# First two attentions of two transformer blocks: steps of 128 queries of two heads instead of one

## What is computed

```python
# fox: forgetting attention, c = cumsum(log f)
s = einsum(q_i, k) * D ** -0.5 + c_q - c_k ; s = where(k_pos <= q_pos, s, NEG_INF)
o_f = softmax(s) @ v
# chunked: chunks of 64 queries, each sees itself and 8 chunks before, with a bias by distance
s = einsum(q_c, k_band) * D ** -0.5 + rel_bias[:, clip(dist)] ; s = where(valid, s, NEG_INF)
o_c = softmax(s) @ v_band
mix = concat([rms_norm(o_f), rms_norm(o_c)]) @ w_out ; x = x + rms_norm(mix)
```

## Time and profile before

| | |
|---|---|
| median of 3 executions | 1573.37 us (1571.94 to 1575.12) |
| the profiled execution | 1575.11 us, its span 1573.3 us |
| PE busy | 1535.1 us, 98% of the span |
| weight loads (PEld) | 1248.9 us, 79% |
| DVE, ACT, POOL busy | 882.4, 593.8, 245.8 us |
| mean granted clock of PE | 0.993 |
| chain that ended last | 87% of it on PE |

### The profile page before, as it was taken

One profiled execution on the slowest core, in us unless ns is written; L12 is line 12 of the kernel. 1 busy time (PEld: TensorE's weight loads), 2 busy tenths in 40 slices (PEclk: granted clock), 3 DMA queues, 4 the chain that ended last, 5 costly groups with the idle time before them and its releaser, 6 DMA issues.

```text
span 1573.3 us, 22000 instructions
## 1 busy us (share of the span) xinstructions
PE 1535.1 (98%) x7988; PEld 1248.9 (79%) x7988; DVE 882.4 (56%) x1239; ACT 593.8 (38%) x889; POOL 245.8 (16%) x273
## 2 busy tenths in 40 slices
PE   9999999999999999999999999999999999999998
PEld 6787766886887788888888678888887788888887
DVE  6434787536452644343332876747877766767323
ACT  6223434544243422222222642334764433334222
POOL 0200000015002300000000455555452000000000
PEclk9999999999999999999999999999999999999999
DMA  5532000521202232333323122322002233332321
GB/s 165 188 101 86 1 2 28 180 88 59 76 28 81 80 104 83 107 90 97 107 82 105 54 81 81 101 86 84 26 1 81 80 106 97 89 107 81 108 106 54
DMA packets 152809, 132.22 MB, mean 84 GB/s; under 512 B 6301, under 2 KB 137629, under 8 KB 152741
## 3 DMA queue, kind: packets, MB, share of 16 engines
q1 hardware_dynamic: 150836, 128.11, 26.4%
q0 software_dynamic: 848, 3.17, 0.6%
q10 hardware_dynamic: 1056, 0.00, 0.0%
HBM read 129.15 MB, written 2.12 MB: 83 GB/s over the span
## 4 chain that ended last, share of the span: by engine, by line
PE 87%; DVE 6%; ACT 2%; POOL 2%; issue 2%; DVEq 0%; ACTq 0%; POOLq 0%
PE ps L1769 24%; PE ps L1771 24%; PE ps L1770 24%; PE ps L2022 2%; PE ps L438 2%; POOL x_t L744 2%; DVE work L1259 1%; PE ps L2014 1%; PE ps L471 1%; PE ps L2033 1%; PE ps L573 1%; PE ps L2155 1%; DVE a_lo L1280 1%; DVE work L1358 1%; PE ps L1957 1%
## 5 line engine op out<-in xcount | busy, mean ns | idle before, releaser
L1769 PE MATMUL ps<-a_hi,w_hi 128*128 128x512 f32 (+2 forms) x1656 | 644.8, 389 | 14.0 <-DVE a_lo L1280 5.0
L1771 PE MATMUL ps<-a_hi,w_lo 128*128 128x512 f32 (+2 forms) x1656 | 639.8, 386 | 0.0
L1770 PE MATMUL ps<-a_lo,w_hi 128*128 128x512 f32 (+2 forms) x1656 | 639.6, 386 | 0.0
L1769 PEld LDWEIGHTS ps<-a_hi,w_hi 128*128 128x128 f32 (+1 forms) x1656 | 311.3, 188 | 86.7 <-issue 10.3
L1771 PEld LDWEIGHTS ps<-a_hi,w_lo 128*128 128x128 f32 (+1 forms) x1656 | 311.2, 188 | 64.1
L1770 PEld LDWEIGHTS ps<-a_lo,w_hi 128*128 128x128 f32 (+1 forms) x1656 | 311.3, 188 | 62.2 <-issue 0.7
L822 ACT ACTIVATE w_hi<-raw 128x2048 fp32r<-128x2048 f32 x118 | 225.8, 1913 | 345.9 <-PE ps L1771 344.1
L1232 DVE TENSOR_TENSOR w_lo<-raw,w_hi 128x2048 fp32r<-128x2048 f32 x94 | 215.2, 2290 | 245.4 <-ACT w_hi L822 245.1
L749 POOL TENSOR_TENSOR w_lo<-raw,w_hi 128x2048 fp32r<-128x2048 f32 x24 | 110.6, 4610 | 449.7 <-ACT w_hi L822 449.7
L1626 DVE TENSOR_TENSOR arena<-ps,rstd 128x512 f32<-128x512 f32 x88 | 60.1, 689 | 166.3 <-PE ps L1771 160.0
L1696 DVE RECIPROCAL rstd<-std 128x512 f32<-128x512 f32 x24 | 80.5, 3353 | 27.2 <-ACT std L1146 27.2
(11 more groups left out here) (235 smaller groups left out, 1538.1 us busy)
## 6 DMA issues: line engine op xcount, KB each, us to landing
raw<-in_w_gate_up SPq DMA_DIRECT2D x44, 512.0 KB, 4.7
raw<-in_ffn_w_up SPq DMA_DIRECT2D x44, 512.0 KB, 4.6
raw<-in_attn_w_in SPq DMA_DIRECT2D x36, 512.0 KB, 4.3
raw<-in_w_in SPq DMA_DIRECT2D x24, 512.0 KB, 4.7
raw<-in_w_down SPq DMA_DIRECT2D x22, 512.0 KB, 4.0
raw<-in_ffn_w_down SPq DMA_DIRECT2D x22, 512.0 KB, 4.1
raw<-in_w_mem_kv SPq DMA_DIRECT2D x16, 512.0 KB, 4.2
raw<-in_w_out SPq DMA_DIRECT2D x8, 512.0 KB, 3.9
```

What stands on the lines that cost most here:

```text
L1769: pe.matmul(dst, s_hi, m_hi, start=start, stop=False, skip_group_check=across)
L1770: pe.matmul(dst, s_hi, m_lo, start=False, stop=False, skip_group_check=across)
L1771: return pe.matmul(dst, s_lo, m_hi, start=False, stop=stop, skip_group_check=across)
```

## The change

A step is now 128 queries of both heads of a pair (`HeadPair`), and both attentions are one list of 32 steps, `PAIRS`, written out on every engine.

- Scores: each head's matmul has 64 rows, its own half of the partitions, and needs no padded queries; the two outputs go to two neighbouring banks. In FOX the decay is added by two matmuls of 64 rows, one for each head (`decay` now stands in rows 0, 32 and again 64, 96, and `sel_pair` replaces `sel_pad`), and the mask by two of 128 rows.
- DVE: one maximum for both heads in FOX, two fused adds in CHUNKED that read the bias where it lies; one inverse and one output product for both heads. It copies only the first head's transposes.
- ACT: two exponentials a step, and the copy of the second head's transposes (`second_out`).
- One step's scores may run two steps ahead; transposes have the banks 6 and 7 for the two heads and no second pair of banks.
- The factor 0.125 of the queries moves into the product behind the query and key tiles (now with a scalar), whose first turn is written out in both projections. The selectors are made by four selects on POOL instead of two, and PE and ACT start on five signals of the constants, not six. POOL's pad copies and its cleared pad are gone. ACT and DVE make the decay's second copy.

```diff
+        class HeadPair:
...
+                self.n, self.slot = (self.i + 1) * 128, 2 * (b % 2)
...
+                self.rows = (slice(0, 64), slice(64, 128))
+                self.scores = ps[:, 4:6, 0:self.n] if b % 2 == 0 else ps[:, 0:2, 0:self.n]
...
+                self.turned = ps[:, 6:8, 0:self.n]
...
@@ POOL
-            pool.affine_select(out=sel_col[:, :], in_=sel_col[:, :], compare_op=ALU.not_equal, fill=-1.0,
-                               base=0, pattern=[[-1, HEADS]], channel_multiplier=1).then_inc(const_step, 1)
...
+            for n, row in enumerate((0, 32, 65, 97)):
...
-            pool.memset(q_pad_1, 0.0).then_inc(pad_1_cleared, 1)
...
@@ ACT
+            act.activation(sel_pair, sel_col[:, :], ACT.Copy).then_inc(decay_ready, 1)
...
+            act.activation(decay[64:72, :], decay_made, ACT.Copy).then_inc(decay_ready, 1)
...
+            def pair_exps(t):
+
+                act.wait_ge(max_done, CREDIT + t.b + 1)
+                if t.b >= 2:
+                    act.wait_ge(turned, CREDIT + t.b - 1)
+                    act.wait_ge(recip_done, CREDIT + t.b - 1)
+                for half in range(2):
...
+            def second_out(t):
+
+                act.wait_ge(turned, CREDIT + t.b + 1)
+                act.wait_ge(values_done, CREDIT + t.b)
+                act.activation(t.probs_t[:, 1, :], t.turned[:, 1, :], ACT.Copy).then_inc(second_read, 1)
+
+            pair_exps(PAIRS[0]), pair_exps(PAIRS[1])
+            for t in PAIRS:
+                second_out(t)
+                if t.b + 2 < BLOCKS:
+                    pair_exps(PAIRS[t.b + 2])
...
@@ DVE
-                        dve.tensor_tensor(flat(ch.c * (2 * S) + (QK_1 + (first + j) * S), S), ps[:, (ch.o * 2 + j) % 4, :],
-                                          rstd[:, :], ALU.mult).then_inc(freed["dve"], 1)
-                over_chunks(dve, G[name], body, peel=int(split_ahead))
+                        dve.scalar_tensor_tensor(out=flat(ch.c * (2 * S) + (QK_1 + (first + j) * S), S),
+                                                 in0=ps[:, (ch.o * 2 + j) % 4, :], scalar=0.125 if ch.o < 2 else 1.0,
+                                                 in1=rstd[:, :], op0=ALU.mult, op1=ALU.mult).then_inc(freed["dve"], 1)
+                over_chunks(dve, G[name], body, peel=1)
...
+            pair_maxima(PAIRS[0]), pair_maxima(PAIRS[1])
+            for t in PAIRS:
+                if t.b:
+                    pair_out(PAIRS[t.b - 1])
+                first_out(t)
+                if t.b + 2 < BLOCKS:
+                    pair_maxima(PAIRS[t.b + 2])
+            pair_out(PAIRS[-1])
...
@@ PE
+            def pair_scores(t):
+
+                if t.b >= 2:
+                    pe.wait_ge(probs_done, CREDIT + t.b - 1)
+                for half, rows in enumerate(t.rows):
+                    last = pe.matmul(t.scores[:, half, :], arena[rows, t.q:t.q + 128], arena[rows, t.k:t.k + t.n],
+                                     start=True, stop=not t.decays)
+                if t.decays:
+                    for half, rows in enumerate(t.rows):
+                        pe.matmul(t.scores[:, half, :], sel_pair[rows, t.p:t.p + 1].to_broadcast([64, 128]),
+                                  decay[rows, 0:t.n], start=False, stop=False)
+                    for half in range(2):
+                        last = pe.matmul(t.scores[:, half, t.n - 128:t.n], ident_r[:, :], causal, start=False, stop=True)
+                last.then_inc(scores_done, 1)
...
+            def pair_values(t):
+
+                pe.wait_ge(turned_read, CREDIT + t.b + 1)
+                pe.wait_ge(second_read, t.b + 1)
+                pe.wait_ge(heads_done, CREDIT + t.b)
...
+            pair_scores(PAIRS[0]), pair_scores(PAIRS[1])
+            for t in PAIRS:
+                pair_turned(t)
+                if t.b + 2 < BLOCKS:
+                    pair_scores(PAIRS[t.b + 2])
+                pair_values(t)
```

More of the change, by code:

```diff
@@ L419, in pipeline @@
                     values(self.pairs - 1, 7)
[L421 to L449, removed]
-            def value(self, p, u, b):
-                return flat(p * 128 + (V_1 + (self.v + b) * HW + u // 4 * 64), 64)
-            def out(self, p, u):
-                return flat(p * 128 + (HEADS_1 + u % 4 * D + self.to + u // 4 * 64), 64)
@@ L707, in _ @@
                     .then_inc(mem_loaded, 16)
-            pool.wait_ge(vec_turned, 1)
-            pool.memset(q_pad_1, 0.0).then_inc(pad_1_cleared, 1)
-            pool.wait_ge(scores_done, CREDIT + 32)
-            with pool.Fori(0, HEADS // 2) as p:
-                for half in range(2):
-                    pool.wait_ge(max_done, p * 8 + (CHUNKED.base + 4 * half - 4))
-                    pool.tensor_copy(rel_pad[:, half, :], flat(p * (2 * S) + (REL + half * S), S))\
-                        .then_inc(rel_padded, 1)
-            pool.wait_ge(max_done, CREDIT + 64)
+            pool.wait_ge(max_done, CREDIT + BLOCKS)
             pool.memset(masks_made, 0.0).then_inc(mask_step, 1)
@@ L1372, in f @@
                         pad(units, p + 1, u // 4)
-                    elif u % 4 == 2 - units.ahead and units is FOX:
-                        pad(CHUNKED, 0, u // 4)
                 return f
@@ L1559, in _ @@
             splits("chunk_v")
-            dve.wait_ge(pad_1_cleared, 1)
-            dve.wait_ge(freed["dve"], CREDIT + G["fox_qk"].freed_end)
-            for half in range(2):
-                pad(FOX, 0, half)
             for f in range(KT):
@@ L2008, in f @@
                     n = units.number(p, u)
-                    if units is FOX and isinstance(p, int) and p == 0:
-                        pe.wait_ge(turns["mem"].read, KT)
                     pe.wait_ge(probs_done, n + 1)
@@ L2030, in f @@
                     blocks = units.keys(u) // 128
-                    if units is MEMORY:
-                        for b in range(blocks):
-                            last = pe.matmul(ps[:, 2 + u % 2, 0:units.width], units.probs_t(u)[:, b * 128:(b + 1) * 128],
-                                             units.value(p, u, b), start=b == 0, stop=b == blocks - 1)
-                    else:
-                        for b in range(blocks):
-                            last = by_column_group(ps[:, 2 + u % 2, 0:units.width],
-                                                   units.probs_t(u)[:, b * 128:(b + 1) * 128], units.value(p, u, b),
-                                                   b == 0, b == blocks - 1)
+                    for b in range(blocks):
+                        last = pe.matmul(ps[:, 2 + u % 2, 0:units.width], units.probs_t(u)[:, b * 128:(b + 1) * 128],
+                                         units.value(p, u, b), start=b == 0, stop=b == blocks - 1)
                     last.then_inc(values_done, 1)
```

135 lines of the change are left out of this document (88 added, 47 removed).

## The result

The changed kernel takes 1560.74 us (median of 4 runs, 1559.58 to 1563.09) against 1573.46 for the kernel before beside it: ratio 0.9922, 95% interval 0.9906 to 0.9938. That is 12.7 us less, where 7.5 was forecast.

| part | before | after | gained | forecast |
|---|---|---|---|---|
| first score starts at | 157.85 | 157.23 | 0.6 | 0 |
| four decay periods | 4 x 13.48 | 4 x 11.75 | 6.9 | 3.3 |
| four chunked periods | 4 x 12.85 | 4 x 10.68 | 8.7 | 5.4 |
| rest of the stage, up to the memory keys | 3.9 | 6.7 | -2.9 | -1.2 |
| everything behind | | | -1.3 | 0 |

What follows compares the result with a forecast made beforehand. TensorE was taken to bound both attentions. Gains of 3.3 (decay) and 5.4 (chunked) less 1.2 at the ends made 7.5 us: 1573.4 to 1565.9, own range 1563 to 1569.5, eight-in-ten range 1558.5 to 1575.0.

Steps and rivals of the forecast that it cites:

- The passes of the scores: TensorE's scores: three records of time for four, so 7 passes a block with decay and 6 chunked, against 10 and 8.
- The rival of whole overlap: Row halves overlap whole, five and four passes; periods 11.7 and 10.8, gain 14, total 1559.3; chance 0.12.
- The sign set for this: Two-head 512-column score, first record to decay or next operation: 1.3 us for three records, 0.9 whole overlap, 1.7 none.
- The changes of division: TensorE switching how its array is divided: four per decay step, three per chunked, each 0.10 to 0.15 us.
- The rival of dearer changes: Array division changes alone cost more: 0.20 each makes the gain 4.7, 0.285 ends it; chance 0.05 beyond 0.20.
- the serial heads: Row halves don't run side by side: about 1574.5, or 1577.5 at 0.20 per change of division; chance 0.14.
- The waits: TensorE waits for ScalarE's second-head copy: 1.3 us per decay period, 2.3 per chunked period.
- The decay loop: From transposes done through next scores, maximum, exponentials and ScalarE's copy to values: 5.5 us against TensorE's 4.2.
- The ends: Stage's start as before; last step's two-head copies and eight uncovered value blocks cost 1.2 us more, bounds -0.5 and 2.5.
- Every later stage as long as before: Sign behind the attention stage: memory keys start at about 259.5 instead of 267.0, and later stages keep their lengths.
- The rival of a falling clock: TensorE's longer waits drop its clock once a period: 13.6 us lost, 6 us slower, 1579.5; chance 0.07.
- the edits at nothing: Moved 0.125, removed pads and pad copies, selector and decay copies, GpSimd's selects: counted as no gain or loss.

Runs made afterwards that it cites:

- e1_same_half: Changed kernel with both heads' score and decay matmuls on one row half (second head's output wrong): 1586.17 us, ratio 1.0075 to the kernel before.
- e5_mask_halves: Changed kernel with the causal mask added by 64-row matmuls on each head's own row half: 1554.04 us, ratio 0.9873 to the kernel before.
- e9_changed_again: The changed kernel itself, no edit, profiled once more with five rounds: 1561.40 us, ratio 0.9920 to the kernel before.
- e8_same_half_clock: Changed kernel with both heads' scores and decays on one row half, and TensorE's waits ahead of the stage filled with unread matmuls: 1579.25 us, ratio 1.0031.
- e6: Changed kernel with ScalarE's copy between the next step's exponentials, mask on row halves, and unread matmuls filling waits before the first score: 1550.69 us, ratio 0.9849.
- e7: Changed kernel with ScalarE's copy between the next step's exponentials and the mask on row halves, without filling matmuls: 1549.93 us, ratio 0.9851.
- e10: Changed kernel with copy between exponentials, mask on halves, odd and even steps' values in two banks, so VectorE copies first: 1549.62 us, ratio 0.9846.

## Why the prediction was right in its direction and short in its size

The forecast named the right bound, the right loop and the right wait, and mis-sized four terms. Over the stage they are worth:

- **The passes of the scores, the main one.** The sum had 7 and 6 passes for a block, on the rule that two records of one head keep the other head's from running until they are through. The step that failed is that rule, taken from the column halves of the earlier trace rows. Score to mask takes 0.49, 0.74, 1.02 and 1.29 us for 128 to 512 keys, 0.22 + 0.267k, and 0.267 is five passes of 0.0533; the forecast's terms make 1.75 of the last. Chunked, TensorE's 8.88 fits four passes. Two passes of 0.0533 less on ten blocks are 1.07 a period, 8.5 us in all. The rival of whole overlap, given 0.12, was the case. That its periods of 11.7 and 10.8 stand so close to 11.75 and 10.68, and its 1559.3 to 1560.7, is in part luck: it kept the forecast's changes and waits, whose errors (the next two points, -5.4 and +3.7) largely cancel. What the Trainium skill, TensorE: Matmul & The Clock Gate, Part 3, says of packed tiles holds here for plain-float scores of two records a head, with 7 ns between the heads' starts. The forecast named it and set it below a reading of rows that showed no row halves. e1_same_half bounds the other end: without overlap 2.4 and 1.7 us a period more.

  The sign set for this would have misled. The forecast read it from the first score record to the decay's, 1.3 for its three records and 0.9 for whole overlap. But the decay's first record starts 0.56 behind the scores', as it does in before (181.79 to 182.35). The 1.29 above is up to the mask, one pass further, and its nearness to 1.3 means nothing.
- **The changes of division, dearer.** With five passes TensorE's own decay period is 10.88 = 10 x 0.721 + 4 x 0.92, where the forecast had 0.77 for a step's fixed parts; chunked 8.88 = 10 x 0.667 + 4 x 0.55, against 0.365. That is -5.4 us. The starts show where: mask to values takes 0.37 (0.45 for 512 keys) where 0.26 was reckoned, transposes to scores 0.15 + 0.22k for 0.10 + 0.22k. That it is the changes of division is shown for one of them, 0.2 by e5_mask_halves; the rest is what a fit leaves. The rival of dearer changes had the direction, and the overlap hid it. Its price was half of what it should be: 16 steps with four changes and 16 with three are 112, so each 0.01 costs 1.12 us and not 0.56. By its own terms 0.20 would have left a gain of 1.9, not 4.7, and 0.217 would have ended it; the 1577.5 of the serial heads has the same slip.
- **The waits, shorter.** 0.87 and 1.80 against 1.3 and 2.3: +3.7. The place was exact in the decay half (ahead of the values of 384 keys, behind the exponentials of 512). In the chunked half the longer wait, 0.95, stands one step earlier, ahead of the values of 256 keys. The decay loop is 4.96 (177.88 to 182.84) where 5.5 was reckoned. The scores have about half of that (1.74 up to the values for 2.0), the two exponentials 0.1 (1.34 for 1.45).
- **The ends.** -2.9 against -1.2. The forecast said the start would be as before; in the profiled execution the half clock lasted 10 us. Without that fall (e9_changed_again) the stage is 3.8 shorter, and the ends would have been a gain of 0.9 on before's, which has a fall of its own.

7.5 + 8.5 - 5.4 + 3.7 - 1.7 = 12.6, where the stage gained 12.7. The 12.7 of the medians is the same figure by chance, since the executions differ in where the clock falls. Outside the stage, 0.5 at the program's start was not forecast: the text said that the first matmuls no longer wait for the last select, and took it for nothing because the input blocks arrive later. "Every later stage as long as before" is off by 1.3 in the profiled execution, with the clock's falls in other places; medians can't be split this way.

The rival of a falling clock did not come about. Waits of 0.9 to 1.1 once or twice a period let the clock stand at 1.00 in both traces of the changed kernel. Its premise is not refuted for waits of 2.0: the one of 1.97 in e8_same_half_clock was followed by a fall, the one of 1.98 in e1_same_half was not. In the profiled execution the falls behind the stage come after waits of 0.77, 2.47 and 2.38 (ahead of 348.6, 497.8 and 1164.0), and the one at 158 after 1.37 and 0.44.

Right were the order of magnitude of both halves of the gain, the second head's copy as the new wait, VectorE no longer the second bound, and the edits at nothing: with the gain at the program's start taken off, the first score stands where it stood, within 0.15.

Open is why the programs with the mask on halves have a better clock. Their 18 runs (e5, e6, e7, e10) have a mean clock of 0.9957, the 9 of the changed kernel 0.9930. The difference is 4 us of full-speed work, about what e5's median gained beyond its stage; its four runs are few. Untested is what leaving out the pads, their copies and the padded selector is worth by itself: it is part of the gain, and no run puts them back.

## What to carry to other kernels

Two matmuls of 64 rows on the two row halves cost the time of one, also when each is a plain float32 product of two records; what eats into it is every change between whole, row-half and column-half matmuls, so a small whole-array matmul in between should be rewritten for the halves. When a second engine is given half of a copy, put the copy between that engine's long instructions and not behind them, and try the single longer copy first: one instruction on an engine that waits may be cheaper than a fair split. A profile with a clock fall in the stage under study is to be taken again before a few microseconds in it are explained, and one profile without it proves nothing about the edit that was made.

## What the runs showed of the hardware that I had not expected

- The whole overlap of row halves for two-record float32 matmuls: 1.29 us for two heads on two halves, with their records 7 ns apart, 2.37 on one.
- One change of division less (row halves to column halves straight, and not by way of the whole array): 0.2 us.
- How long the clock stays at half once it has fallen: 3.5, 10 and 24 us in three programs with ever fewer rows of the array at work, with TensorE busy throughout; and that the median stays when the waits ahead of it are filled (1561.5 against 1560.7 and 1561.4), though that trace has no fall in the stage.
- The same program, and the same wait in two programs, with a fall of the clock behind it in one execution and none in another (158 in after and e9_changed_again; 1.97 and 1.98 in e8_same_half_clock and e1_same_half).
